# A two-block transformer step: three last blocks turned on VectorE and by DMAs instead of on TensorE

## The chip, the cores and the metric

One NeuronCore of a Trainium2 chip runs one launch of the program. The metric is the device time of the launch in microseconds (us), the median of several runs. The engines are TensorE (PE in the profile, PEld its weight loads), VectorE (DVE), ScalarE (ACT), GpSimd (POOL) and SyncE (SP, which only issues DMAs and waits).

## The reference

The input x has 256 tokens of width 2048, in float32. Two blocks follow each other. Cut to what matters here:

```
# first block
h = rms_norm(x) ;  proj = h @ w_in            # four mixers over proj, 512 columns each
x1 = x + rms_norm_per_mixer(mixed) @ w_out
h = rms_norm(x1, norm_ffn)                    # x1 * rstd * norm_ffn
x2 = x1 + (silu(h @ w_gate) * (h @ w_up)) @ w_down       # 5632 inner columns
# second block
o = attention(x2 @ attn_w_in)                 # x2 enters without a norm
x3 = layer_norm(ALPHA * x2 + (o * silu(g)) @ attn_w_out)
o = retention(x3 @ ret_w_in)                  # 8 heads, 512 value columns each
o = group_norm_per_head(o) * silu(g)
out = layer_norm(ALPHA * x3 + o @ ret_w_out)  # 4096 x 2048
```

Each of x1 * norm_ffn, x2 and o * silu(g) is computed with tokens on the partitions and must be the transposed operand of the next product, with its features on the partitions. They must be turned, block by block of 512 columns (a head of the retention is one such block).

## The kernel before

**Products.** The program is a chain of phases: in1, out1, ffn (11 bodies of 8 chunks), down, in2, out2, ret (4 bodies of 24 chunks), out3. In each, an output block of 512 columns (256 tokens, so two banks of PSUM, `ACC`) is summed over chunks of 512 input rows of the weights. A chunk (1 MB) is loaded by SP into one of four places of `raw`. It is used in two halves. To keep float32 accuracy, each half is split: ScalarE copies it to the shorter type fp32r (`split_hi`, `whi`, L379), VectorE subtracts that from the original (`split_lo`, `wlo`, L386), and TensorE makes three products in place of one (`products`, L406 to L408): 12 matmuls of 512 columns for a half. The other operand lies turned in SBUF, split in the same way (`T1H` and `T1L` for ffn and in2, `T2dH` and `T2dL` for out3).

**Order.** Each engine has its own queue, written out by hand and run in order; semaphores tie them. `whi` and `wlo` have places for four halves, so `split_hi` of half q waits until TensorE has finished half q-4, `split_lo` waits for `split_hi`, and a half's products wait for its `split_lo`. SP loads a chunk when VectorE has split the chunk four before it. The other work of each engine is put between the splits, at a position given by the half's number h (or p). What stands "at h" on ScalarE or VectorE comes behind the split of half h.

**Two ways of turning a block.** The first is TensorE's: `tr_pe` makes four transposes of 128x128 for each of the two token groups into a PSUM bank (L439), `tr_act` copies the bank to the high part (L444), `tr_dve` subtracts for the low part (L448). The second leaves TensorE out: VectorE transposes squares of 32x32 within the block (`dve.transpose`, two instructions, into `sg` or `oS`), then 16 DMAs of 32 KB carry the squares between partition groups (`group_across`, L460, four DMAs for each of r = 0 to 3) into `avT` or `oT`; ScalarE copies the turned block to the high part (`x1_hi`, `turned_hi`), VectorE subtracts for the low part (`x1_lo`, `turned_lo`). The semaphore `sq_dve` counts three for each block turned in this way: two for the squares, one for the low part. `sq_in` and `o_in` count landed DMAs.

**Where each is used.** Of the four blocks of x1, blocks 0 to 2 go the second way with the DMAs on GpSimd's queue; of the four of x2, blocks 0 to 2 with the DMAs on SP's, four before each of four weight loads; so do heads 0 to 6 of the retention. Block 3 of x1, block 3 of x2 and head 7 go the first way: their `tr_pe` stands in TensorE's queue behind half 1 of ffn's first body, behind half 1 of in2 and behind half 5 of out3, which are already products with the blocks before. The products with the last block begin at half 6 of ffn and in2 and at half 14 of out3, where TensorE waits for `tb_done`.

Of the kernel before, what the change touches and what calls it, by code (L numbers as in the profile page):

```python
# [33 lines left out]
P = 128  # L34
# [34 lines left out]
ACROSS = 4 * 4 * 16  # L69
SQ = {"mix": 0, "out1": 2, "ffn": 5, "down": 16, "in2": 19, "ret": 21}  # L70
BY_SP = {"ffn": 0, "down": 11, "ret": 14}

# [20 lines left out]
def two_blocks(nc, A, out):  # L93
# [133 lines left out]
    SML = at("SML", G0 + 18 * KB, [P, 2, T], F32R)  # L227
    oR = at("oR", G0 + 24 * KB, [P, J, W])
    gR = at("gR", G0 + 28 * KB, [P, J, W])
    X4 = at("X4", G0, [P, J, D])  # L230
# [46 lines left out]
    def sem(name):  # L277
# [46 lines left out]
        sem(x) for x in ("r_sq", "r_hi", "r_S", "r_SM", "r_out", "r_ms", "r_rs", "r_norm", "r_og", "r_TL", "r_vH", "r_prod", "r_SMH"))  # L324
    x4_ready, out_st = sem("x4_ready"), sem("out_st")

# [189 lines left out]
    BLK = {"in1": 0, "out1": 11, "ffn": 15, "down": 37, "in2": 41, "out2": 51, "ret": 55, "out3": 79}  # L516
    TB = {"mix": 0, "out1": 4, "down": 6, "in2": 8, "out2": 12, "ret": 20}

# [80 lines left out]
    def _(sp):  # L599
# [29 lines left out]
        for c in range(8):  # L629
            w = A["w_ffn_gate"] if c < 4 else A["w_ffn_up"]  # L630
            load(sp, "ffn", c, [(0, W, chunk(w[0], c % 4, 0))])
        with sp.Fori(1, NF) as f:
# [59 lines left out]
        with sp.Fori(1, RH // 2) as i:  # L692
            ret(i, False)
        for c in range(32):
            load(sp, "out3", c, [(0, W, chunk(A["ret_w_out_2"][0], c % 8, c // 8 * W))])
        n = 0
# [10 lines left out]
    def _(pool):  # L707
# [125 lines left out]
        for hd in range(RH):  # L833
            pool.wait_ge(r_sq, 2 * hd + 2)
            for r in range(2, 4):
                group_across(pool, line3(rb), line4(rTs), r, t_in2)
        pool.wait_ge(tb_done, TB["ret"] + 2)
        pool.dma_start(lnG2[:, :], spread(A["ln_gain_2"][1], D)).then_inc(ln_in, 16)
# [9 lines left out]
    def _(act):  # L848
# [211 lines left out]
        def x1_hi(b):  # L1060
            act.wait_ge(o_in, (b + 1) * ACROSS)
            act.activation(by_token(T1H[:, 4 * b:4 * b + 4, :]), avT[:, :, :, :], ACT.Copy).then_inc(sq_hi, 1)

        for b in range(FB):
            for h in range(8):
                split_hi(act, "out1", 4 * b + h // 2, h % 2)
                if b == 0:
                    if h == 1:
                        mix_rstd(2)
                    if h == 2:  # L1070
                        out1_block(NB1 - 1)
                    mix_hi(h)
                    if h == 3:
                        act.wait_ge(oc_ready, NH)
                        squares(3)
                    if h == 4:
                        mix_rstd(3)
                if b and h == 4:
                    x1_squares(b - 1)
                if b >= 2 and h == 3:  # L1080
                    x1_hi(b - 2)


        def ffn(f, first):
            for h in range(16):
                split_hi(act, "ffn", h // 2, h % 2, i=f)
                if first and h == 2:
                    x1_squares(FB - 1)
                if first and h == 3:
                    x1_hi(2)  # L1090
                    for j in range(J):
                        tr_act(act, TB["out1"] + j, part(T1H, 3, j), k=j)
                if first and h == 4:
                    rstd(rstd2, ms1, 3, rs1)
                    table_silu()
                if not first and h == 13:
                    turned_hi(act, f - 1, T2bH[:, bass.ds(f * 4 - 4, 4), :], avT, f)
                if first and h == 11:

                    act.wait_ge(x1_st[0], 32)  # L1100
                    act.wait_ge(x1_st[1], 32)
                if h == 11:
                    block_done(act, "ffn", 3, f)
                    if not first:

                        act.wait_ge(sq_in, f * ACROSS)
                    for j in range(J):
                        act.activation(sg[:, j, :], ACC[BLK["ffn"] % 2][j], ACT.Silu, scale=rstd2[:, j:j + 1]).then_inc(acc_out[BLK["ffn"] % 2], 1)
# [191 lines left out]
        for b in range(FB):  # L1300
            for h in range(16):
# [4 lines left out]
                if b == 0 and h == 3:  # L1306
# [15 lines left out]
    def _(dve):  # L1322
# [281 lines left out]
        def x1_block(b):  # L1604
# [10 lines left out]
            tt(xgb[:, b % 2, :, :], x1b[:, b % 2, :, :], rep(gF[:, b * W:(b + 1) * W], 0, J), MUL).then_inc(xg2, 1)  # L1615
            if b < FB - 1:
                dve.wait_ge(xg2, b + 1)
                if b:
                    dve.wait_ge(o_in, b * ACROSS)
                for j in range(J):  # L1620
                    dve.transpose(sg[:, j, :], xgb[:, b % 2, j, :]).then_inc(sq_dve, 1)

# [4 lines left out]
        for b in range(FB):  # L1627
            for h in range(8):
# [15 lines left out]
                if b and h == 3:  # L1644
                    x1_block(b - 1)


# [17 lines left out]
        def ffn(f, first):  # L1665
            for h in range(16):
# [26 lines left out]
        def x2_block(b):  # L1693
# [5 lines left out]
            for j in range(J):  # L1699
                tt(x2b[:, j, :], ACC[B % 2][j], xr2[:, j, :], ADD).then_inc(acc_out[B % 2], 1)  # L1700
            if b < FB - 1:
                for j in range(J):
                    dve.wait_ge(acc_out[B % 2], 2 * (B // 2) + 1 + j)
                    dve.transpose(sg[:, j, :], x2b[:, j, :]).then_inc(sq_dve, 1)

# [40 lines left out]
        def in2_at(p):  # L1746
            if p == 0:
                x2_block(FB - 1)
            if p == 3:
                for j in range(J):  # L1750
                    tr_dve(dve, TB["down"] + j, part(T1H, 3, j), part(T1L, 3, j), k=j)
            if p == 7:
# [302 lines left out]
        for b in range(FB):  # L2055
            for h in range(16):
# [5 lines left out]
                if b == 0 and h == 4:  # L2062
# [25 lines left out]
    def _(pe):  # L2088
# [219 lines left out]

        def x1_tr(b):
            pe.wait_ge(xg2, b + 1)  # L2310
            for j in range(J):
                tr_pe(pe, TB["out1"] + j, xgb[:, b % 2, j, :], k=j)

        for b in range(FB):
# [10 lines left out]
        def ffn(f, first):  # L2325
            for h in range(16):
                if first and h == 0:
                    pe.wait_ge(sq_dve, 3 * (SQ["ffn"] - 1))
                if first and h == 4:
                    pe.wait_ge(sq_dve, 3 * SQ["ffn"])  # L2330
                if first and h == 6:
                    pe.wait_ge(tb_done, TB["out1"] + 2)
                products(pe, "ffn", h // 2, h % 2, T1H, T1L, 4 * (h % 8 // 2), BLK["ffn"] + h // 8, W, h % 8 == 0, h % 8 == 7, f)
                if first and h == 1:
                    x1_tr(FB - 1)

# [3 lines left out]


        def x2_tr():
            B = BLK["down"] + FB - 1
            pe.wait_ge(acc_out[B % 2], 2 * (B // 2) + 2)
            for j in range(J):
                tr_pe(pe, TB["down"] + j, x2b[:, j, :], k=j)

# [42 lines left out]
        for p in range(80):  # L2390
            b, h = p // 8, p % 8
            if p == 0:
                pe.wait_ge(sq_dve, 3 * SQ["in2"])
            if p == 6:
                pe.wait_ge(tb_done, TB["down"] + 2)
            products(pe, "in2", p // 2, p % 2, T1H, T1L, 4 * (h // 2), BLK["in2"] + b, W, h == 0, h == 7)
            if p == 1:
                x2_tr()
            in2_at(p)
# [83 lines left out]
        for b in range(FB):  # L2483
            for h in range(16):
                if b == 0 and h == 0:
                    pe.wait_ge(sq_dve, 3 * (SQ["ret"] + RH - 1))
                if b == 0 and h == 14:
                    pe.wait_ge(tb_done, TB["ret"] + 2)
                if b == FB - 1 and h >= 16 - 2 * SPLITS:
                    continue  # L2490
                products(pe, "out3", 8 * b + h // 2, h % 2, T2dH, T2dL, 4 * (h // 2), BLK["out3"] + b, W, h == 0, h == 15)
                if b == 0 and h == 5:
                    pe.wait_ge(r_og, 2 * RH)
                    for j in range(J):
                        tr_pe(pe, TB["ret"] + j, oR[:, j, :], (4, 6), j)
        b = FB - 1
# [79 lines left out]
```

## Time and profile before

| | us |
|---|---|
| median of 3 runs (2189.58 to 2190.57) | 2189.77 |
| span of the profiled execution, first to last instruction | 2187.9 |
| TensorE busy, share of the span | 2175.2, 99% |
| VectorE busy | 1341.7, 61% |
| ScalarE busy | 1039.5, 48% |
| GpSimd busy | 222.5, 10% |
| from HBM | 415.32 MB, 194 GB/s over the span with 8.39 MB written |

The profile gives the profiled execution's own time only as its span; the median of the runs lies 1.9 us above it. Matmuls are pipelined and their ends are modelled, so a busy TensorE is not one at its peak: the distance from one matmul's start to the next tells more. Times of the rows count from the start of the span.

### The profile page before, as it was taken

Reading aid. Unit: us, or ns where it says so; the run is one execution under the profiler, and the core shown is the slowest. Engines: PE = TensorE matmul, PEld = TensorE weight load, DVE = VectorE, ACT = ScalarE, POOL = GpSimd, SP = SyncE. Lnnn points to the kernel's source line nnn. Section 1 sums busy time; section 2 is a strip of 40 time slices with the busy share of each in tenths; the row PEclk is TensorE's granted clock in tenths of the full one; section 3 lists DMA queues with packets and bytes.
Section 4 is the critical chain, followed back from the end, with each engine's and each line's share of the span. In section 5 each row is a group of like instructions: output and inputs, shape, how many; then the busy total and the mean of one; then the engine's idle time right before and its main releaser. Section 6 shows DMA issues by size and latency. Waiting matters only on the chain.

```text
span 2187.9 us, 26695 instructions
## 1 busy us (share of the span) xinstructions
PE 2175.2 (99%) x9999; PEld 1809.9 (83%) x9999; DVE 1341.7 (61%) x1645; ACT 1039.5 (48%) x1292; POOL 222.5 (10%) x376
## 2 busy tenths in 40 slices
PE   9999999999999999999999999999999999999998
PEld 7888888888888888888888888888888888888886
DVE  6675676555555555445566776587666565665556
ACT  6554664444444444444444455445444544544333
POOL 1012015000000000010002352000000000000000
PEclk9999999999999999999999999999999999999999
DMA  9557568676657665676766776757676657756763
GB/s 317 194 162 200 163 221 283 198 217 214 201 184 224 206 201 185 219 227 222 223 210 205 202 211 198 269 197 222 188 212 192 200 186 209 211 170 200 257 204 111
DMA packets 388375, 454.83 MB, mean 208 GB/s; under 512 B 167042, under 2 KB 202274, under 8 KB 387137
## 3 DMA queue, kind: packets, MB, share of 16 engines
q1 hardware_dynamic: 371568, 414.97, 60.6%
q0 software_dynamic: 16432, 38.43, 5.9%
q8 instruction: 55, 0.90, 0.2%
q10 hardware_dynamic: 288, 0.27, 0.0%
q14 instruction: 32, 0.25, 0.0%
HBM read 415.32 MB, written 8.39 MB: 194 GB/s over the span
## 4 chain that ended last, share of the span: by engine, by line
PE 99%; DVE 0%; DMA 0%; SPq 0%; ACT 0%; issue 0%
PE bank L406 30%; PE bank L408 30%; PE bank L407 30%; PE bank L420 1%; PE bank L422 1%; PE bank L421 1%; PE bank L2381 1%; PE bank L2368 1%; PE bank L2154 0%; PE bank L439 0%; PE bank L2477 0%; PE bank L2478 0%; PE bank L2476 0%; PE bank L2139 0%; DMA raw<-in_w_in 0%; PE bank L2218 0%
## 5 line engine op out<-in xcount | busy, mean ns | idle before, releaser
L386 DVE TENSOR_TENSOR wlo<-raw,whi 128x1024 fp32r<-128x1024 f32 x749 | 903.6, 1216 | 681.2 <-ACT whi L379 679.7
L379 ACT ACTIVATE whi<-raw 128x1024 fp32r<-128x1024 f32 x749 | 780.4, 1053 | 777.1 <-PE bank L408 761.3
L406 PE MATMUL bank<-whi,T1H 128*128 128x512 f32 (+1 forms) x2100 | 823.7, 392 | 0.0
L408 PE MATMUL bank<-whi,T1L 128*128 128x512 f32 (+1 forms) x2100 | 814.7, 388 | 0.0
L407 PE MATMUL bank<-wlo,T1H 128*128 128x512 f32 (+1 forms) x2100 | 814.1, 388 | 0.0
L408 PEld LDWEIGHTS bank<-whi,T1L 128*128 128x128 f32 x2100 | 394.2, 188 | 81.6
L406 PEld LDWEIGHTS bank<-whi,T1H 128*128 128x128 f32 x2100 | 394.4, 188 | 79.6 <-DVE wlo L386 0.2
L407 PEld LDWEIGHTS bank<-wlo,T1H 128*128 128x128 f32 x2100 | 394.5, 188 | 79.3
L406 PE MATMUL bank<-whi,T2bH 128*128 128x512 f32 x352 | 136.9, 389 | 0.0
L407 PE MATMUL bank<-wlo,T2bH 128*128 128x512 f32 x352 | 136.9, 389 | 0.0
L408 PE MATMUL bank<-whi,T2bL 128*128 128x512 f32 x352 | 136.9, 389 | 0.0
L406 PE MATMUL bank<-whi,T2dH 128*128 128x512 f32 x224 | 87.2, 389 | 0.0
L408 PE MATMUL bank<-whi,T2dL 128*128 128x512 f32 x224 | 87.1, 389 | 0.0
L407 PE MATMUL bank<-wlo,T2dH 128*128 128x512 f32 x224 | 87.1, 389 | 0.0
L460 POOL DMA_DIRECT2D rTs<-rb x64 | 37.2, 588 | 468.7 <-DVE rb L1999 462.4
L408 PEld LDWEIGHTS bank<-whi,T2bL 128*128 128x128 f32 x352 | 66.1, 188 | 13.8
L407 PEld LDWEIGHTS bank<-wlo,T2bH 128*128 128x128 f32 x352 | 66.1, 188 | 13.7
L406 PEld LDWEIGHTS bank<-whi,T2bH 128*128 128x128 f32 x352 | 66.1, 188 | 13.6
L790 POOL DMA_DIRECT2D scr_x<-x2b x4 | 2.9, 723 | 648.3 <-DVE x2b L1700 648.3
L406 PE MATMUL bank<-whi,T2aH 128*128 128x512 f32 x128 | 50.3, 393 | 0.0
L408 PE MATMUL bank<-whi,T2aL 128*128 128x512 f32 x128 | 49.9, 390 | 0.0
L407 PE MATMUL bank<-wlo,T2aH 128*128 128x512 f32 x128 | 49.8, 389 | 0.0
(406 smaller groups left out, 1843.7 us busy)
## 6 DMA issues: line engine op xcount, KB each, us to landing
raw<-in_ret_w_in SPq DMA_DIRECT2D x64, 1024.0 KB, 5.4
raw<-in_w_ffn_gate SPq DMA_DIRECT2D x44, 1024.0 KB, 5.2
raw<-in_w_ffn_up SPq DMA_DIRECT2D x44, 1024.0 KB, 5.6
raw<-in_w_ffn_down SPq DMA_DIRECT2D x44, 1024.0 KB, 5.7
raw<-in_attn_w_in SPq DMA_DIRECT2D x40, 1024.0 KB, 5.4
raw<-in_w_in SPq DMA_DIRECT2D x39, 1024.0 KB, 5.1
raw<-in_ret_w_in SPq DMA_DIRECT2D x64, 512.0 KB, 4.6
raw<-in_ret_w_out SPq DMA_DIRECT2D x32, 1024.0 KB, 5.1
```

What stands on the lines that cost most here:

```text
L379: eng.activation(hi_[:, s, :, :n], raw[:, c % RAWS, HALF * hf:HALF * (hf + 1), :n], ACT.Copy).then_inc(hi_ready, 1)
L386: eng.tensor_tensor(lo[:, s, :, :n], raw[:, c % RAWS, HALF * hf:HALF * (hf + 1), :n], hi_[:, s, :, :n].bitcast(F32), ALU.subtract).then_in ...
L406: eng.matmul(o, TH[:, kt, xs], hi_[:, s, t, :n], start=first and t == 0, stop=False)
L407: eng.matmul(o, TH[:, kt, xs], lo[:, s, t, :n], start=False, stop=False)
L408: m = eng.matmul(o, TL[:, kt, xs], hi_[:, s, t, :n], start=False, stop=last and t == HALF - 1)
L420: eng.matmul(o, TH[:, kt, xs], hi_[:, s, t, :], start=first and t == 0, stop=False)
L421: eng.matmul(o, TH[:, kt, xs], lo[:, s, t, :], start=False, stop=False)
L422: m = eng.matmul(o, TL[:, kt, xs], hi_[:, s, t, :], start=False, stop=last and t == HALF - 1)
L460: eng.dma_start(dst[:, :, r, :], src[:, :, b, :]).then_inc(landed_, 16)
L790: pool.dma_start(rows(scr_x2)[:, :, cs], x2b[:, :, :]).then_inc(x2_st, 16)
L2368: m = mm(bank[6][:, j * T:(j + 1) * T], qTa[:, g % 2, j, a, :], kTa[:, :, g, :], start=True, stop=True)
L2381: m = mm(bank[(5, 7)[u % 2]][:, j * P:(j + 1) * P], PTa[u // 2 % 2][:, u % 2, j, s, :], vA[:, s, g * P:(g + 1) * P], start=s == 0, stop=s ...
```

## The change

Block 3 of x1, block 3 of x2 and head 7 of the retention are turned the second way. Their `tr_pe`, `tr_act` and `tr_dve` go. VectorE makes the squares behind the block's sum. SP issues all 16 DMAs of a block in one row: ahead of the load of chunk 4 in ffn's first body and in in2, and of chunk 7 in out3. For x1 they count on a semaphore of their own, `x1z_in`. To keep the order of `sq_dve`, the copy and the subtraction of x1's block 2 move from half 3 of ffn's first body to behind the split of out1's last half, and those of block 3 stand at half 3. For x2 the copy stays at p = 3, the subtraction goes to p = 4. For the retention head the squares stand at half 5, copy and subtraction at half 10, and two new tiles, `oSz` and `oTz`, take the squares and the turned block. GpSimd's loads for the last layer norm wait for head 7's subtraction as before, now by `sq_dve`.

```
-SQ = {"mix": 0, "out1": 2, "ffn": 5, "down": 16, "in2": 19, "ret": 21}
-BY_SP = {"ffn": 0, "down": 11, "ret": 14}
+SQ = {"mix": 0, "out1": 2, "ffn": 6, "down": 17, "in2": 21, "ret": 23}
+BY_SP = {"ffn": 0, "down": 11, "ret": 15}
...
+    oSz = at("oSz", G0 + 32 * KB, [P, J, W])
+    oTz = at("oTz", G0 + 36 * KB, [P, J, 4, P])
...
@@ SP
         for c in range(8):
             w = A["w_ffn_gate"] if c < 4 else A["w_ffn_up"]
+            if c == 4:
+                sp.wait_ge(sq_dve, 3 * (SQ["out1"] + FB - 1) + 2)
+                for r in range(4):
+                    group_across(sp, line3(sg), line4(avT), r, x1z_in)
             load(sp, "ffn", c, [(0, W, chunk(w[0], c % 4, 0))])
...
             for cc in range(4):
+                if 4 * b + cc == 4:
+                    for r in range(4):
+                        block_across(sp, SQ["down"] + FB - 1, sg, avT, r)
                 load(sp, "in2", 4 * b + cc, [(0, W, chunk(A["attn_w_in_2"][0], cc, COL2[kind] + g * W))])
...
         for c in range(32):
+            if c == 7:
+                for r in range(4):
+                    block_across(sp, SQ["ret"] + RH - 1, oSz, oTz, r)
             load(sp, "out3", c, [(0, W, chunk(A["ret_w_out_2"][0], c % 8, c // 8 * W))])
@@ GpSimd
-        pool.wait_ge(tb_done, TB["ret"] + 2)
+        pool.wait_ge(sq_dve, 3 * (SQ["ret"] + RH))
@@ ScalarE
         def x1_hi(b):
-            act.wait_ge(o_in, (b + 1) * ACROSS)
+            if b == FB - 1:
+                act.wait_ge(x1z_in, ACROSS)
+            else:
+                act.wait_ge(o_in, (b + 1) * ACROSS)
...
                 if b >= 2 and h == 3:
                     x1_hi(b - 2)
+                if b == FB - 1 and h == 7:
+                    x1_hi(2)
...
                 if first and h == 3:
-                    x1_hi(2)
-                    for j in range(J):
-                        tr_act(act, TB["out1"] + j, part(T1H, 3, j), k=j)
+                    x1_hi(FB - 1)
...
             if p == 3:
-                for j in range(J):
-                    tr_act(act, TB["down"] + j, part(T1H, 3, j), k=j)
+                turned_hi(act, SQ["down"] + FB - 1, T1H[:, 4 * FB - 4:4 * FB, :], avT, BY_SP["down"] + FB)
...
-                if b == 0 and h == 7:
-                    for j in range(J):
-                        tr_act(act, TB["ret"] + j, part(T2dH, RH - 1, j), (4, 6), j)
+                if b == 0 and h == 10:
+                    turned_hi(act, SQ["ret"] + RH - 1, T2dH[:, 4 * RH - 4:4 * RH, :], oTz, BY_SP["ret"] + RH)
@@ VectorE
-            if b < FB - 1:
-                dve.wait_ge(xg2, b + 1)
-                ...
+            dve.wait_ge(xg2, b + 1)
+            if b:
+                dve.wait_ge(o_in, b * ACROSS)
+            for j in range(J):
+                dve.transpose(sg[:, j, :], xgb[:, b % 2, j, :]).then_inc(sq_dve, 1)
...
+                if b == FB - 1 and h == 7:
+                    x1_lo(2)
...
                 if first and h == 3:
-                    x1_lo(2)
-                    for j in range(J):
-                        tr_dve(dve, TB["out1"] + j, part(T1H, 3, j), part(T1L, 3, j), k=j)
+                    x1_lo(FB - 1)
...
-            if b < FB - 1:
-                for j in range(J):
-                    ...
+            for j in range(J):
+                dve.wait_ge(acc_out[B % 2], 2 * (B // 2) + 1 + j)
+                dve.transpose(sg[:, j, :], x2b[:, j, :]).then_inc(sq_dve, 1)
...
-            if p == 3:
-                for j in range(J):
-                    tr_dve(dve, TB["down"] + j, part(T1H, 3, j), part(T1L, 3, j), k=j)
+            if p == 4:
+                turned_lo(dve, SQ["down"] + FB - 1, T1H[:, 4 * FB - 4:4 * FB, :], T1L[:, 4 * FB - 4:4 * FB, :], avT)
...
-                if b == 0 and h == 7:
+                if b == 0 and h == 5:
                     for j in range(J):
-                        tr_dve(dve, TB["ret"] + j, part(T2dH, RH - 1, j), part(T2dL, RH - 1, j), (4, 6), j)
+                        dve.wait_ge(r_og, 2 * RH - 1 + j)
+                        dve.transpose(oSz[:, j, :], oR[:, j, :]).then_inc(sq_dve, 1)
+                if b == 0 and h == 10:
+                    turned_lo(dve, SQ["ret"] + RH - 1, T2dH[:, 4 * RH - 4:4 * RH, :], T2dL[:, 4 * RH - 4:4 * RH, :], oTz)
@@ TensorE: x1_tr, x2_tr and the tr_pe of oR go, and
                 if first and h == 6:
-                    pe.wait_ge(tb_done, TB["out1"] + 2)
...
+                if first and h in (0, 4, 6):
+                    pe.wait_ge(sq_dve, 3 * (SQ["ffn"] - {0: 2, 4: 1, 6: 0}[h]))
...
             if p == 0:
+                pe.wait_ge(sq_dve, 3 * (SQ["in2"] - 1))
+            if p == 6:
                 pe.wait_ge(sq_dve, 3 * SQ["in2"])
-            if p == 6:
-                pe.wait_ge(tb_done, TB["down"] + 2)
...
                 if b == 0 and h == 14:
-                    pe.wait_ge(tb_done, TB["ret"] + 2)
+                    pe.wait_ge(sq_dve, 3 * (SQ["ret"] + RH))
```

## Rows read from the trace of the kernel before

**Rows 1.** The page's first part: busy us, share of the span, instructions.

```profile
PE 2175.2 (99%) x9999; PEld 1809.9 (83%) x9999; DVE 1341.7 (61%) x1645; ACT 1039.5 (48%) x1292; POOL 222.5 (10%) x376
```

**Rows 2.** TensorE's waits, all of them: us in total, times, longest.

```profile
PE bank L2300 <- DVE warm L1581: 1.5, 1, 1.5
PE bank L2114 <- DVE wlo L1578: 0.6, 1, 0.6
```

**Rows 3.** TensorE's timeline around x1's transposes: start, us, instruction, count.

```profile
386.50 0.39 PE L406 MATMUL bank<-whi,T1H 128*128 128x512 f32 x1
...
391.71 0.39 PE L408 MATMUL bank<-whi,T1L 128*128 128x512 f32 x1
391.94 1.03 PE L439 MATMUL bank<-cst,xgb 128*128 128x128 f32 x8
...
395.81 0.39 PE L407 MATMUL bank<-wlo,T1H 128*128 128x512 f32 x1
```

**Rows 4.** ScalarE's timeline, same place: two splits and block 2's copy.

```profile
375.82 1.06 ACT L379 ACTIVATE whi<-raw 128x1024 fp32r<-128x1024 f32 x1 [1.60 <-PE bank L408]
...
384.04 1.06 ACT L379 ACTIVATE whi<-raw 128x1024 fp32r<-128x1024 f32 x1 [1.72 <-PE bank L408]
...
390.59 1.04 ACT L1062 ACTIVATE T1H<-avT 128x1024 fp32r<-128x1024 f32 x1
```

**Rows 5.** VectorE's timeline: block 2's sum, squares, splits, block 3's sum.

```profile
368.31 1.28 DVE L1612 TENSOR_TENSOR x1b<-bank,xrb 128x512 f32<-128x512 f32 x2
...
370.89 1.31 DVE L1621 STREAM_TRANSPOSE sg<-xgb 128x512 f32<-128x512 f32 x2
372.12 3.46 DVE L386 TENSOR_TENSOR wlo<-raw,whi 128x1024 fp32r<-128x1024 f32 x3
...
386.70 1.29 DVE L1612 TENSOR_TENSOR x1b<-bank,xrb 128x512 f32<-128x512 f32 x2 [3.12 <-PE bank L408]
```

**Rows 6.** Block 2's last DMAs on GpSimd's queue, and their landing.

```profile
L460 POOL DMA_DIRECT2D avT<-sg x2: 585/585/585, 380.7 to 381.3; - x2
DMA to landing us min/median/max: 4.2/4.5/4.8
```

**Rows 7.** SP's timeline: a weight load, eight small DMAs, four beside loads; landings; the load's median.

```profile
383.61 0.37 SPq L365 DMA_DIRECT2D raw<-in_w_ffn_up  x1
...
1146.17 5.19 SPq L460 DMA_DIRECT2D qTa<-tS  x8
DMA to landing us min/median/max: 1.9/2.1/2.9
...
1058.23 3.77 SPq L460 DMA_DIRECT2D avT<-sg  x4
DMA to landing us min/median/max: 3.0/4.3/5.0
...
raw<-in_w_ffn_up SPq DMA_DIRECT2D x44, 1024.0 KB, 5.6
```

**Rows 8.** Timelines of VectorE, ScalarE and TensorE where in2 begins.

```profile
1105.70 1.29 DVE L1700 TENSOR_TENSOR x2b<-bank,xr 128x512 f32<-128x512 f32 x2 [5.78 <-PE bank L408]
1105.70 1.06 ACT L379 ACTIVATE whi<-raw 128x1024 fp32r<-128x1024 f32 x1 [1.60 <-PE bank L408]
1108.22 0.45 PE L406 MATMUL bank<-whi,T1H 128*128 128x512 f32 x1
```

**Rows 9.** Timelines of VectorE and TensorE in out3's first block.

```profile
2010.28 1.22 DVE L386 TENSOR_TENSOR wlo<-raw,whi 128x1024 fp32r<-128x1024 f32 x1
2018.69 1.03 PE L439 MATMUL bank<-cst,oR 128*128 128x128 f32 x8
```

**Rows 10.** Warm-up matmuls (ns min/median/max, starts), and windows: granted clock after PE's busy time.

```profile
L2300 PE MATMUL bank<-warm x6: 592/866/1222, 1.5 to 5.1; 128*128 128x512 f32 x6
...
2178.00:2180.00 2.00, 0.00 (x0) 1.00 0.00 0
2182.00:2182.20 0.20, 0.00 (x0) 0.64 0.97 369
```

More of the change, by code:

```diff
@@ L324, in two_blocks @@
         sem(x) for x in ("r_sq", "r_hi", "r_S", "r_SM", "r_out", "r_ms", "r_rs", "r_norm", "r_og", "r_TL", "r_vH", "r_prod", "r_SMH"))
-    x4_ready, out_st = sem("x4_ready"), sem("out_st")
+    x4_ready, out_st, x1z_in = sem("x4_ready"), sem("out_st"), sem("x1z_in")
     class Chain:
@@ L516, in two_blocks @@
     BLK = {"in1": 0, "out1": 11, "ffn": 15, "down": 37, "in2": 41, "out2": 51, "ret": 55, "out3": 79}
-    TB = {"mix": 0, "out1": 4, "down": 6, "in2": 8, "out2": 12, "ret": 20}
+    TB = {"mix": 0, "out1": 4, "in2": 4, "out2": 8}
     def where1(c):
@@ L1615, in x1_block @@
             tt(xgb[:, b % 2, :, :], x1b[:, b % 2, :, :], rep(gF[:, b * W:(b + 1) * W], 0, J), MUL).then_inc(xg2, 1)
-            if b < FB - 1:
-                dve.wait_ge(xg2, b + 1)
-                if b:
-                    dve.wait_ge(o_in, b * ACROSS)
-                for j in range(J):
-                    dve.transpose(sg[:, j, :], xgb[:, b % 2, j, :]).then_inc(sq_dve, 1)
+            dve.wait_ge(xg2, b + 1)
[3 more added lines that the diff above has]
+                dve.transpose(sg[:, j, :], xgb[:, b % 2, j, :]).then_inc(sq_dve, 1)
         def x1_lo(b):
@@ L1700, in x2_block @@
                 tt(x2b[:, j, :], ACC[B % 2][j], xr2[:, j, :], ADD).then_inc(acc_out[B % 2], 1)
-            if b < FB - 1:
-                for j in range(J):
-                    dve.wait_ge(acc_out[B % 2], 2 * (B // 2) + 1 + j)
-                    dve.transpose(sg[:, j, :], x2b[:, j, :]).then_inc(sq_dve, 1)
+            for j in range(J):
+                dve.wait_ge(acc_out[B % 2], 2 * (B // 2) + 1 + j)
+                dve.transpose(sg[:, j, :], x2b[:, j, :]).then_inc(sq_dve, 1)
         for b in range(FB):
@@ L1748, in in2_at @@
                 x2_block(FB - 1)
-            if p == 3:
-                for j in range(J):
-                    tr_dve(dve, TB["down"] + j, part(T1H, 3, j), part(T1L, 3, j), k=j)
+            if p == 4:
+                turned_lo(dve, SQ["down"] + FB - 1, T1H[:, 4 * FB - 4:4 * FB, :], T1L[:, 4 * FB - 4:4 * FB, :], avT)
             if p == 7:
@@ L2306, in _ @@
             mix_tr(p - 8 * NB1)
[L2309 to L2312, printed above, removed]
         for b in range(FB):
@@ L2326, in ffn @@
             for h in range(16):
[L2327 to L2331, printed above, removed]
-                    pe.wait_ge(tb_done, TB["out1"] + 2)
+                if first and h in (0, 4, 6):
+                    pe.wait_ge(sq_dve, 3 * (SQ["ffn"] - {0: 2, 4: 1, 6: 0}[h]))
                 products(pe, "ffn", h // 2, h % 2, T1H, T1L, 4 * (h % 8 // 2), BLK["ffn"] + h // 8, W, h % 8 == 0, h % 8 == 7, f)
-                if first and h == 1:
-                    x1_tr(FB - 1)
         ffn(0, True)
@@ L2339, in _ @@
             ffn(f, False)
[L2342 to L2346, printed above, removed]
         for b in range(FB):
@@ L2392, in _ @@
             if p == 0:
+                pe.wait_ge(sq_dve, 3 * (SQ["in2"] - 1))
+            if p == 6:
                 pe.wait_ge(sq_dve, 3 * SQ["in2"])
-            if p == 6:
-                pe.wait_ge(tb_done, TB["down"] + 2)
             products(pe, "in2", p // 2, p % 2, T1H, T1L, 4 * (h // 2), BLK["in2"] + b, W, h == 0, h == 7)
-            if p == 1:
-                x2_tr()
             in2_at(p)
@@ L2491, in _ @@
                 products(pe, "out3", 8 * b + h // 2, h % 2, T2dH, T2dL, 4 * (h // 2), BLK["out3"] + b, W, h == 0, h == 15)
[L2492 to L2495, printed above, removed]
         b = FB - 1
```

## The prediction, made before the changed kernel was run

> **What bounds the kernel now.** I read the page's first part, then TensorE's waits, then the timeline of each engine around the three places that change. TensorE is busy for 99% of the span [rows 1], but that share is modelled, so the second view matters more: in the whole execution it waits twice, 2.1 us in all, both at the start [rows 2]. The timeline says the same in another way. From 386.50 to 391.71 there are 24 matmul starts, 0.2265 us apart [rows 3], and this spacing holds nearly everywhere. A half chunk is 12 matmuls, so 2.72 us. So everything that leaves TensorE's stream is won, and everything that makes a half's `wlo` late is lost.
>
> How near is that lateness? `whi`/`wlo` hold four halves. ScalarE's split of half q waits until TensorE has finished q-4, VectorE's follows, and both queues are in order. Between blocks these engines idle, so they look free; but whatever stops one of them for more than about three halves (8 us), less its own work, stops TensorE. That is the measure for all that follows.
>
> **What leaves TensorE.** Eight transposes at each of three places. At x1, 391.71 to 395.81 is 4.10 us [rows 3]; the 14 intervals without the transposes would take 3.17, so they cost 0.93. The other two groups have the same shape (1.03 us for eight in [rows 9]), so I take 0.9 each: 2.7 us in all, 0.12% of the time. That is the most the change can give. What is gone from ScalarE and VectorE (two half-size copies and two subtractions each) is replaced by one full-size copy (1.04) and one subtraction (1.22), and counts as nothing: on those engines it is the same amount of work and lies between splits.
>
> **Place A, x1.** Three waits come in, in a row.
>
> First, block 2. Its copy `x1_hi(2)` moves from half 3 of the ffn phase to behind the split of out1's last half, which ScalarE issues at 375.82 [rows 4]. There it waits for GpSimd's 16 DMAs, whose last is issued at 381.3 and lands 4.2 to 4.8 us later [rows 6]: 385.8. Before, it ran at 390.59 with nothing to wait for [rows 4]. Behind it on ScalarE stand the splits of ffn halves 0, 1 and 2, which had run ahead (the third at 384.04). So: copy to 386.85, split 0 (1.06) to 387.9; on VectorE `x1_lo(2)` to 388.1, `wlo` 0 (1.23) to 389.3. TensorE started that half at 386.50 [rows 3], so it stands 2.8 us. `wlo` 1 ends at 390.5.
>
> Second, block 3's squares. `x1_block(3)` started at 386.70 and now starts at 390.5. With transposes it takes 3.81 us to the next split (368.31 to 372.12, block 2) [rows 5], so `wlo` 2 ends at 395.5. TensorE has gone through halves 0 and 1 by 389.3 + 5.4 = 394.7: 0.8 us more.
>
> Third, the DMAs. SP waits for the squares, 3.9 us after 390.5, at 394.4, and issues 16 DMAs before the load of chunk 4. Eight such issues take 5.19 us, 0.65 each, and land in 1.9 to 2.9 (median 2.1) where no weight load is under way [rows 7]; here the loads before have landed and the next stand behind. Last issue starts 15 x 0.65 = 9.75 later, landing at 406.3. ScalarE has stood in `x1_hi(3)` since split 3, and split 4 is queued behind it: copy to 407.3, split to 408.4; `x1_lo(3)` to 408.5 and `wlo` 4 to 409.7 on VectorE. TensorE has finished half 3 at 401.0 and stands for 8.7 us. Before, half 4 began at 395.81 + 11 x 0.2265 = 398.3. Place A: +11.4 us, the saved transposes included. Chunk 4 is issued at about 405 instead of 383.61 and its half 8 is wanted four halves after 409.7, at 420; a load lands in 5.6 us [rows 7], so that is covered.
>
> **Place B, x2.** `x2_block(3)` starts at 1105.70 on VectorE [rows 8], and TensorE's half 1 began at 1108.22, just behind its `wlo`. Two transposes (1.31) [rows 5] before that split make it late by about 1.3. SP starts at 1105.70 + 1.29 + 1.31 = 1108.3; the last DMA starts at 1118.0 and lands at 1120.1. ScalarE had issued split 3 at 1105.70 [rows 8] and now stands in the copy, splits 4 and on behind it. Copy to 1121.2, split 4 to 1122.3, `wlo` 4 to 1123.5 (`turned_lo` comes after it here). Before, half 4 began at 1108.22 + 36 x 0.2265 + 0.9 for the transposes = 1117.3. Place B: +6.2 us, of which 5.9 is one stand.
>
> **Place C, the retention head.** `wlo` of half 5 runs at 2010.28 [rows 9]; the squares follow to 2012.8, the DMAs in quiet land at 2012.8 + 9.75 + 2.1 = 2024.7. The copy stands behind split 10, and TensorE wants half 11 at 2018.69 + 5 x 2.72 = 2032.3; the copy, the subtraction and `wlo` 11 take 3.5, so a landing before 2028.8 costs nothing. That is 4 us of room: -0.9. But chunk 6 is being loaded just then. With a load beside them four issues took 3.77 (0.94 each) and landed up to 5.0 us later [rows 7]; so 2031.9, and 3.1 us lost. I take the first; the second is a bound.
>
> **The clock.** After its last matmul TensorE was still granted full clock in 2178 to 2180, and the clock fell near 2182.1 [rows 10], with no matmul in between. At the start the same plain fp32 matmul record is 592 to 1222 ns, and the slow ones run from 1.48 to some 4.3 us [rows 10]. So stands of 8.7 and 5.9 us can bring 1.2 GHz, and about 2.8 us of work then goes at half speed, losing 1.4 each time: +2.8. Bounds: nothing, if the clock stays, and 2 us each. The Trainium skill ("TensorE: Matmul & The Clock Gate", "Part 1: The HAM clock gate") has the same two levels, with idle time lowering the clock and sustained work restoring it; by it both stands cost as the rows say, and a sum without it is 2.8 lower.
>
> **Sum.** 11.4 + 6.2 - 0.9 + 2.8 = +19.5 us. Span 2187.9 + 19.5 = 2207.4. The profile gives no time of that execution but its span; the median of the runs lies 1.9 above, and I keep that: 2209.3, slower by 0.89%.
>
> **Rivals.**
> *All covered (0.04).* The DMAs land before the copies need them. For B this needs a landing by 1114.2, 6 us after the squares; for A 2.9 us after them, and block 2 by 383. Against it: 16 issues alone take 9 to 10 us. Even then B keeps its 1.3 us of transposes ahead of `wlo` 1 against the 0.9 saved: -0.9 + 0.4 - 0.9 - a rest near zero gives 2188.4. Not slower, and within what a measurement tells.
> *Cheap issues (0.06).* SP's issue of a weight load takes 0.37 [rows 7]. If the small ones, queued 16 in a row, went at that pace, the last starts 5.6 after the squares: A +7.2, B +2.0, C -0.9, and the clock perhaps once: 2189.8 + 8.3 + 1.4 = 2199.5. Against it are the eight in 5.19. The Trainium skill ("DMA: Bandwidth & Descriptors", "Issuing engines are not separate DMA queues") goes further: issuing is usually small beside the DMA itself. Taken so, only the landing would count, A would be about +2.5 and B +0.4, in all 2191.8; the rows have 0.65 per issue, sixteen times, against one landing of 2.1, so they disagree with it.
> *Crowded DMAs (0.12).* 0.94 per issue and 5 us of landing at all three places: A and B +7.3 each, C +4.0: 2228 at the very most; a part of it is likelier, 2217 to 2222. For it: such rows exist; against it: at A and B the loads are held back by the same SP queue. GpSimd's store of the block (512 KB) is the only other traffic.
> *Forecast (0.78)*: both places stand on the turning, issues near 0.65, with or without the clock.
>
> **Numbers.** A measurement of this kernel tells about 0.2% (4.4 us) from no change. Within the forecast: no clock loss 2206.5; issues at 0.585 and landing in 1.9 take 1.2 from each place, 2204.1; clock at 2 each and 1.5 us more landing each give 2213.5; a part of C's loss 2216. Range 2203 to 2216: it leaves out the first two rivals and most of the third, at most 2 in 10. Faster would take more than the 2.7 us that exist: 0.01. Same: 0.05. Slower: 0.94.
>
> **What the profile after would show.** No L439 rows with xgb, x2b or oR; L460 on SP with 16 in a row at each place; TensorE's waits with three or four new entries: about 3 us before ffn half 0, 1 before half 2, 9 before half 4 and, in in2, 1.3 before half 1 and 6 before half 4; ScalarE waiting for the DMAs at the copies; a granted clock below 1.00 for a few us after both long stands; nothing at C. I am wrong if the copies find their data landed, if ScalarE's splits reach half 4 without them, or if C shows a wait.

## The result, and the profile after

The changed kernel takes 2210.14 us (median of 4 runs, 2209.7 to 2210.49) against 2189.98 for the kernel before on the same chip: a ratio of 1.0092, 95% interval 1.0079 to 1.0104, 20.2 us. The prediction was 2209.3, range 2203 to 2216. The span went from 2187.9 to 2208.5 us.

The page's first part and TensorE's waits of the kernel after, against [rows 1, 2]:

```profile
PE 2179.0 (99%) x9975; PEld 1810.7 (82%) x9975; DVE 1344.5 (61%) x1648; ACT 1039.0 (47%) x1289; POOL 221.6 (10%) x376
...
PE bank L408 <- DVE wlo L388: 17.6, 4, 8.5
PE bank L2313 <- DVE warm L1594: 1.5, 1, 1.5
```

The busy share still says 99%. The new line of waits says the rest: four times, 17.6 us, TensorE stood for a `wlo`, so for the second half of a weight split, and never for a turned block. So something further back in the queues of ScalarE and VectorE held the splits up. (Of the lines that carry the split and the products before, L379, L386 and L406 to L408 are now L381, L388 and L408 to L410; `group_across` is L462.)

**x1.** TensorE's timeline, against [rows 3]:

```profile
386.42 0.39 PE L410 MATMUL bank<-whi,T2aL 128*128 128x512 f32 x1
388.93 0.47 PE L408 MATMUL bank<-whi,T1H 128*128 128x512 f32 x1 [2.12 <-DVE wlo L388]
...
401.29 0.39 PE L410 MATMUL bank<-whi,T1L 128*128 128x512 f32 x1
410.17 0.76 PE L408 MATMUL bank<-whi,T1H 128*128 128x512 f32 x1 [8.49 <-DVE wlo L388]
410.73 0.63 PE L409 MATMUL bank<-wlo,T1H 128*128 128x512 f32 x1
```

Half 0 of ffn begins at 388.93, half 4 at 410.17. Before, half 4 began at 398.30 and the last matmul of out1 at 386.27:

```profile
386.27 0.39 PE L408 MATMUL bank<-whi,T2aL 128*128 128x512 f32 x1
...
398.30 0.39 PE L406 MATMUL bank<-whi,T1H 128*128 128x512 f32 x1
```

What held it is read backwards, from ScalarE's, VectorE's and SP's timelines (one fence for each; against [rows 4, 5, 7]):

```profile
375.97 1.06 ACT L381 ACTIVATE whi<-raw 128x1024 fp32r<-128x1024 f32 x1 [1.60 <-PE bank L410]
385.33 1.06 ACT L1077 ACTIVATE T1H<-avT 128x1024 fp32r<-128x1024 f32 x1 [8.30 <-DMA avT<-sg]
386.29 2.93 ACT L381 ACTIVATE whi<-raw 128x1024 fp32r<-128x1024 f32 x3
...
392.74 1.06 ACT L381 ACTIVATE whi<-raw 128x1024 fp32r<-128x1024 f32 x1
406.57 1.06 ACT L1077 ACTIVATE T1H<-avT 128x1024 fp32r<-128x1024 f32 x1 [12.77 <-DMA avT<-sg]
407.54 1.04 ACT L381 ACTIVATE whi<-raw 128x1024 fp32r<-128x1024 f32 x1
```

```profile
389.83 1.28 DVE L1625 TENSOR_TENSOR x1b<-bank,xrb 128x512 f32<-128x512 f32 x2
...
407.66 1.23 DVE L485 TENSOR_TENSOR T1L<-avT,T1H 128x1024 fp32r<-128x1024 f32 x1 [11.43 <-ACT T1H L1077]
408.80 1.22 DVE L388 TENSOR_TENSOR wlo<-raw,whi 128x1024 fp32r<-128x1024 f32 x1
```

```profile
393.74 11.50 SPq L462 DMA_DIRECT2D avT<-sg  x16
405.29 9.90 SPq L367 DMA_DIRECT2D raw<-in_w_ffn_up  x4
```

ScalarE waits twice in front of a copy, 8.30 us for block 2's DMAs and 12.77 us for block 3's. Behind the first stand three splits (386.29, x3), behind the second split 4 (407.54), on which `wlo` 4 (408.80) and TensorE (410.17) depend. Between the two copies lie the 16 issues on SP, 11.50 us, from 393.74; a change of order on the other engines doesn't shorten them.

**x2.** VectorE, SP, ScalarE and TensorE where in2 begins, against [rows 8]:

```profile
1119.15 1.29 DVE L1712 TENSOR_TENSOR x2b<-bank,xr 128x512 f32<-128x512 f32 x2 [5.78 <-PE bank L410]
1121.68 10.91 SPq L462 DMA_DIRECT2D avT<-sg  x16
1133.92 1.06 ACT L481 ACTIVATE T1H<-avT 128x1024 fp32r<-128x1024 f32 x1 [13.71 <-DMA avT<-sg]
...
1122.81 0.50 PE L408 MATMUL bank<-whi,T1H 128*128 128x512 f32 x1 [0.98 <-DVE wlo L388]
1137.24 0.79 PE L408 MATMUL bank<-whi,T1H 128*128 128x512 f32 x1 [5.97 <-DVE wlo L388]
```

The same chain, with a short stand before half 1 (the two transposes ahead of `wlo` 1) and the long one before half 4.

**The retention head.** SP's and ScalarE's timelines, VectorE's at the start of out3, and below them the landings from the view of the tile `oTz`:

```profile
2034.23 10.44 SPq L462 DMA_DIRECT2D oTz<-oSz  x16
...
2046.01 1.06 ACT L481 ACTIVATE T2dH<-oTz 128x1024 fp32r<-128x1024 f32 x1 [1.77 <-DMA oTz<-oSz]
...
2021.34 1.23 DVE L388 TENSOR_TENSOR wlo<-raw,whi 128x1024 fp32r<-128x1024 f32 x1
```

```profile
DMA to landing us min/median/max: 1.9/1.9/4.1
```

ScalarE waits 1.77 us there too, but it had run ahead, and TensorE has no wait.

The same instruction in both traces gives the size of each place. TensorE's last matmul of out1 starts 0.15 later than before (386.42 against 386.27). The sum of x2's block 3 starts at 1119.15 against 1105.70, an offset of 13.45: so x1 cost 13.3. The split at 2021.34 stood at 1999.83 before, an offset of 21.51: x2 cost 8.1. At the end the offset is 20.6: the retention head gave 0.9. The split before, in VectorE's timeline:

```profile
1999.83 1.22 DVE L386 TENSOR_TENSOR wlo<-raw,whi 128x1024 fp32r<-128x1024 f32 x1
```

### The profile page after: what moved, and what is told of

It is laid out like the page before. It is cut to its first block, busy times and chain, and to the rows that moved or that the text cites. A ratio compares the mean times of both kernels' runs of the same rounds, so it can differ in the third digit from the quotient of the medians.

```text
span 2208.5 us, 26693 instructions
## 1 busy us (share of the span) xinstructions
PE 2179.0 (99%) x9975; PEld 1810.7 (82%) x9975; DVE 1344.5 (61%) x1648; ACT 1039.0 (47%) x1289; POOL 221.6 (10%) x376
## 4 chain that ended last, share of the span: by engine, by line
PE 97%; DVE 1%; SPq 1%; POOL 0%; DMA 0%; issue 0%; ACT 0%; DVEq 0%; ACTq 0%
PE bank L408 29%; PE bank L410 29%; PE bank L409 29%; SPq L462 1%; PE bank L422 1%; PE bank L424 1%; PE bank L423 1%; PE bank L2377 1%; PE bank L2364 1%; PE bank L2167 0%; POOL avT L462 0%; DMA avT<-sg 0%; PE bank L2472 0%; PE bank L2471 0%; PE bank L2470 0%; PE bank L2152 0%
## 5 line engine op out<-in xcount | busy, mean ns | idle before, releaser
L388 DVE TENSOR_TENSOR wlo<-raw,whi 128x1024 fp32r<-128x1024 f32 x749 | 903.1, 1216 | 686.3 <-ACT whi L381 685.1
L381 ACT ACTIVATE whi<-raw 128x1024 fp32r<-128x1024 f32 x749 | 780.1, 1053 | 774.5 <-PE bank L410 762.1
L408 PE MATMUL bank<-whi,T1H 128*128 128x512 f32 (+1 forms) x2100 | 826.0, 393 | 17.6 <-DVE wlo L388 17.6
L410 PE MATMUL bank<-whi,T1L 128*128 128x512 f32 (+1 forms) x2100 | 816.3, 389 | 0.0
L408 PEld LDWEIGHTS bank<-whi,T1H 128*128 128x128 f32 x2100 | 395.6, 188 | 98.8 <-issue 11.4
L410 PEld LDWEIGHTS bank<-whi,T1L 128*128 128x128 f32 x2100 | 395.0, 188 | 82.3
L408 PE MATMUL bank<-whi,T2bH 128*128 128x512 f32 x352 | 136.9, 389 | 0.0
L410 PE MATMUL bank<-whi,T2bL 128*128 128x512 f32 x352 | 136.9, 389 | 0.0
L408 PE MATMUL bank<-whi,T2dH 128*128 128x512 f32 x224 | 87.1, 389 | 0.0
L410 PE MATMUL bank<-whi,T2dL 128*128 128x512 f32 x224 | 87.1, 389 | 0.0
L462 POOL DMA_DIRECT2D rTs<-rb x64 | 37.0, 586 | 468.7 <-DVE rb L2009 462.5
L408 PEld LDWEIGHTS bank<-whi,T2bH 128*128 128x128 f32 x352 | 66.1, 188 | 13.8
L410 PEld LDWEIGHTS bank<-whi,T2bL 128*128 128x128 f32 x352 | 66.1, 188 | 13.7
L408 PE MATMUL bank<-whi,T2aH 128*128 128x512 f32 x128 | 50.3, 393 | 0.0
L410 PE MATMUL bank<-whi,T2aL 128*128 128x512 f32 x128 | 49.9, 390 | 0.0
```

The source lines that it names most:

```text
L381: eng.activation(hi_[:, s, :, :n], raw[:, c % RAWS, HALF * hf:HALF * (hf + 1), :n], ACT.Copy).then_inc(hi_ready, 1)
L388: eng.tensor_tensor(lo[:, s, :, :n], raw[:, c % RAWS, HALF * hf:HALF * (hf + 1), :n], hi_[:, s, :, :n].bitcast(F32), ALU.subtract).then_in ...
L408: eng.matmul(o, TH[:, kt, xs], hi_[:, s, t, :n], start=first and t == 0, stop=False)
L410: m = eng.matmul(o, TL[:, kt, xs], hi_[:, s, t, :n], start=False, stop=last and t == HALF - 1)
L462: eng.dma_start(dst[:, :, r, :], src[:, :, b, :]).then_inc(landed_, 16)
```

## The experiments

**One place at a time.** Three kernels, each with the new way at one place and TensorE's way at the other two (the counts in `SQ`, `BY_SP` and `TB` go with it). A part of the first, on TensorE, against the kernel after:

```
 # x1 only: x2 and the retention head as in the kernel before
+            if p == 1:
+                B = BLK["down"] + FB - 1
+                pe.wait_ge(acc_out[B % 2], 2 * (B // 2) + 2)
+                for j in range(J):
+                    tr_pe(pe, TB["down"] + j, x2b[:, j, :], k=j)
...
+                if b == 0 and h == 5:
+                    pe.wait_ge(r_og, 2 * RH)
+                    for j in range(J):
+                        tr_pe(pe, TB["ret"] + j, oR[:, j, :], (4, 6), j)
```

> Only block 3 of x1 is turned by squares and DMAs; x2's last block and head 7 are turned by TensorE as before. In the trace after, TensorE had lost 13.3 us between the start of ffn and the end of down (the same VectorE instruction at 1105.70 before and 1119.15 after, less 0.15 of an earlier shift). Theory (the three places are independent, each with its own stand of TensorE): 2190.0 + 13.3 = 2203.3 us. Rival (the places share something, the DMA queue or the clock, so that they don't add): more than 1 us away from that, with the sum of the three single runs away from the whole change's +20.2.

> Only block 3 of x2 is turned by squares and DMAs. In the trace after, this place lost 8.1 us (an offset of 13.45 before it and 21.51 behind it). Theory (independent places): 2190.0 + 8.1 = 2198.1 us. Rival (not independent): more than 1 us away from it.

> Only head 7 of the retention is turned by squares and DMAs. Theory (its turning is wholly hidden, and eight transposes leave TensorE's stream at 0.9 us): 2190.0 - 0.9 = 2189.1 us, no wait of TensorE in out3. Rival (what TensorE no longer does is filled by something else, or the crowded weight loads behind SP's 16 DMAs cost it): 2190.0 or above.

Measured against 2190.0 us: x1 alone 2203.08 (ratio 1.0059, 1.0044 to 1.0075), x2 alone 2198.68 (1.0039, 1.0023 to 1.0054), the head alone 2189.34 (0.9997, 0.9988 to 1.0006). In us: +13.1, +8.7, -0.7. They sum to 21.1 against 20.2 of the whole change, with runs of one kernel up to 2 us apart. The places are independent within that. The head's gain is not told from nothing by its times. That it costs no wait is seen in TensorE's list, which holds the start alone:

```profile
PE bank L2307 <- DVE warm L1585: 1.5, 1, 1.5
```

**The clock.** Only matmuls are added, into a bank that nobody reads:

```
+                if first and h == 4:           # 34 in ffn; the same with 22 at p == 4 in in2
+                    for k in range(34):
+                        pe.matmul(bank[4], T1H[:, 0, 0:P], T1H[:, 2:4, :].rearrange("p a t -> p (a t)"), start=True, stop=True)
                 products(pe, "ffn", h // 2, h % 2, T1H, T1L, ...)
```

> The whole change, and 34 more matmuls of 512 columns on TensorE before ffn's half 4, 22 before in2's half 4, into a bank that nobody reads; they take 7.7 and 5.0 us and fit into the stands of 8.7 and 6.1 us. Theory (of each long stand about 1.65 us is not waiting but work at the lower clock afterwards: eight starts 0.43 apart in place of 0.23): 2210.1 - 3.3 = 2206.8 us, and a granted clock of 1.00 behind both. Rival (the slow matmuls behind the stands cost nothing because VectorE's and ScalarE's catching up sets the pace there anyway): 2210.1.

Measured: 2206.93 us (1.0079, 1.0063 to 1.0094), 3.2 below the change. Windows of TensorE, first after, then this kernel (columns: us, PE busy and count, granted clock, DMA share, GB/s):

```profile
402.00:410.00 8.00, 0.00 (x0) 0.78 0.60 158
410.00:414.00 4.00, 3.83 (x10) 0.58 0.84 282
```

```profile
402.00:410.00 8.00, 6.65 (x29) 1.00 0.65 188
410.00:414.00 4.00, 4.00 (x19) 1.00 0.77 230
```

In the kernel after, the granted clock falls from full to 1.2 GHz (0.50) late in this stand: it is 1.00 in 405.0 to 406.5 and 0.50 from 406.5 on. From 410 to 414 the kernel after holds 10 matmul starts, this one 19. The tenth matmul of half 4 in the kernel after, whose first is at 410.17, then the first and the tenth of this kernel:

```profile
413.78 0.40 PE L408 MATMUL bank<-whi,T1H 128*128 128x512 f32 x1
```

```profile
409.43 0.50 PE L408 MATMUL bank<-whi,T1H 128*128 128x512 f32 x1 [1.35 <-DVE wlo L388]
...
411.61 0.39 PE L408 MATMUL bank<-whi,T1H 128*128 128x512 f32 x1
```

The nine intervals take 3.61 us, and the same 3.61 behind x2's stand (1137.24 to 1140.85); with the clock kept they take 2.18. So the clock costs 1.4 us at each place, 2.9 of the 20.2, and that is not waiting. The spans of the two profiled executions differ by 3.7: the 2.9, and 0.7 by which half 4 itself began sooner (409.43 against 410.17).

**The copies two halves later.** Nothing but the place of two calls on each engine moves:

```
-                if first and h == 3:
+                if first and h == 5:
                     x1_hi(FB - 1)      # ScalarE; x1_lo on VectorE the same
...
-            if p == 3:                 # ScalarE; on VectorE p == 4
+            if p == 5:
```

> The whole change, but ScalarE's copy and VectorE's subtraction of the last block stand at half 5 in ffn's first body and at p = 5 in in2, in place of 3 (and 4). Nothing else moves; TensorE needs the block at half 6. Theory (the stand comes from the splits 4 and 5 queued behind a copy whose data is under way): x1's copy begins with the landing as before (406.5), so TensorE stands before half 6 for 3.2 us in place of 8.7 before half 4, in2's for 0.8 in place of 6.1; with the clock kept 1.65 less each: 2210.1 - 5.5 - 5.3 - 3.3 = 2196 us (2199 if the clock falls anyway). Rival (TensorE stands for its operand, the turned block, and not for the splits): no change, 2210.

Measured: 2198.57 us (1.0038, 1.0025 to 1.0051), 11.6 less than the change. The rival is out: the operand was not what TensorE stood for before half 4. The time lies between the theory's two numbers (2196 with the clock kept, 2199 if it falls). The clock did fall at x1: it is 0.50 in 411.5 to 413.0. ScalarE's copy in its timeline, and TensorE's longest line of waits:

```profile
406.66 1.06 ACT L1077 ACTIVATE T1H<-avT 128x1024 fp32r<-128x1024 f32 x1 [7.84 <-DMA avT<-sg]
```

```profile
PE bank L408 <- DVE wlo L388: 8.7, 5, 4.4
```

The copy runs when it ran before, at 406.66, but splits 4 and 5 are done. The stand before half 6 is 4.4 and not the 3.2 expected, because TensorE came to it sooner: it had no stand before half 4 and, in this execution, no low clock behind the first stand.

**Two queues for the DMAs.**

```
-                for r in range(4):
+                for r in range(2):
                     group_across(sp, line3(sg), line4(avT), r, x1z_in)
...
+        pool.wait_ge(sq_dve, 3 * (SQ["out1"] + FB - 1) + 2)     # GpSimd; x2 alike
+        for r in range(2, 4):
+            group_across(pool, line3(sg), line4(avT), r, o_in)
```

> The whole change, but at x1 and x2 SP issues 8 of the 16 DMAs and GpSimd the other 8. Copies and subtractions stay. Theory (the turning is long because one queue needs 0.65 to 0.7 us for each of 16 issues; the landing is 2 us): the last lands 5 us earlier at both places, so the stands are 3.7 and 1.1 us and the clock may hold: 2210.1 - 10 - 3 = 2197 us (2200 with the clock falling at x1). Rival (the small copies share the same DMA engines, so that issuing them from two queues gives nothing): 2210.

Measured: 2200.91 us (1.0045, 1.0029 to 1.006), 9.2 less, near the 2200 expected if the clock falls at x1, which it did. So most of the turning's length was issue time on the one queue. The copy at x2 runs 9.83 us after the sum's start (1126.01, 1116.18) in place of 14.77, 4.9 sooner as expected; by the offsets x2 gave 6.4 of the time, the clock there being kept, and x1 3.0. At x1 the gain is 2.9 us of landing and not 5. SP's, GpSimd's and ScalarE's timelines there, and the landing of SP's eight:

```profile
393.73 5.70 SPq L462 DMA_DIRECT2D avT<-sg  x8
399.47 10.53 SPq L367 DMA_DIRECT2D raw<-in_w_ffn_up  x3
...
393.99 4.63 POOL L462 DMA_DIRECT2D avT<-sg  x8 [1.87 <-DVE sg L1643]
398.70 0.73 POOL L799 DMA_DIRECT2D xr<-scr_x  x1
...
403.65 1.06 ACT L1085 ACTIVATE T1H<-avT 128x1024 fp32r<-128x1024 f32 x1 [9.86 <-DMA avT<-sg]
```

```profile
DMA to landing us min/median/max: 1.9/2.4/4.8
```

The last of SP's eight starts at 398.8 and lands 4.8 later, beside a weight load (399.47, in the kernel after at 405.29) and GpSimd's load of `xr` (398.70, in the kernel after at 395.11). The one comes sooner because SP has eight issues less ahead of it, the other later because GpSimd has eight more. With all 16 on SP no load ran beside the last ones and they landed in 1.9. That the loads are the cause is argued from the trace; no run takes them away.

**Block 2's copy put back.**

```
-                if b == FB - 1 and h == 7:
-                    x1_hi(2)                # ScalarE; x1_lo(2) on VectorE
...
                 if first and h == 2:
+                    x1_hi(2)
                     x1_squares(FB - 1)
...
                 if first and h == 1:
+                    x1_lo(2)
                     x1_block(FB - 1)
```

> The whole change, but the copy and subtraction of x1's block 2 stand behind the splits of ffn's half 2 (ScalarE) and half 1 (VectorE), in place of behind out1's last split. Theory (this moved step holds three splits, makes a first stand of 2.3 us and starts block 3's squares 1.6 us late): the first stand is gone and the squares come 1.6 us earlier, so that all behind them does: 2210.1 - 1.6 = 2208.5 us. Rival (all stands add, and the first one's 2.3 us with its slow matmuls come back whole): 2206 or less.

Measured: 2209.37 us (1.0089, 1.0074 to 1.0105), 0.8 less, where the theory had 1.6 and the rival 4 or more: the rival is out by the time. The first stand is gone, and half 4 of ffn begins at 407.37 in place of 410.17, 2.8 sooner. The stand before it has grown, though, and the stretch at low clock behind it is longer. TensorE's waits, half 4, and the window behind it:

```profile
PE bank L408 <- DVE wlo L388: 16.4, 4, 9.1
```

```profile
407.37 0.77 PE L408 MATMUL bank<-whi,T1H 128*128 128x512 f32 x1 [9.10 <-DVE wlo L388]
```

```profile
407.00:414.00 7.00, 6.63 (x18) 0.57 0.86 302
```

Thirteen intervals are long there, against seven in the kernel after, and ten against seven behind x2's stand. So of the 2.8 us 1.6 are left by in2 and 0.9 at the end. The 0.8 of the medians is no larger than the spread of the runs. The run also doesn't tell by size what the 2.8 us are: block 3's sum starts 2.4 sooner, and the stand that went was 2.3 long.

**All three repairs.** The above together, and two places more: x1's turned block goes to a place of its own, so that its DMAs start with the squares and need not wait until `avT` is read, and x2's squares stand behind the split of half 1.

```
+    xTz = at("xTz", FT + 8 * KB, [P, J, 4, P])
...
-                sp.wait_ge(sq_dve, 3 * (SQ["out1"] + FB - 1) + 2)
+                sp.wait_ge(sq_dve, 3 * (SQ["out1"] + FB - 1) + 1)
-                for r in range(4):
-                    group_across(sp, line3(sg), line4(avT), r, x1z_in)
+                for r in range(2):
+                    group_across(sp, line3(sg), line4(xTz), r, x1z_in)
...
             if p == 0:
                 x2_block(FB - 1)
+            if p == 1:
+                x2_squares(FB - 1)
```

> The whole change with the three repairs together: DMAs of x1's and x2's last blocks half on SP and half on GpSimd, their copies and subtractions at half 5, block 2's copy at half 2 and subtraction at half 2, x1's turned block in a place of its own so that its DMAs start with the squares, and x2's squares behind the split of half 1. Theory (each turning is then covered by halves 0 to 5, and only the 24 transposes' 2.7 us are left): no wait of TensorE at any of the three places, 2190.0 - 2.6 = 2187.4 us. Rival (some 1 us stand remains at x1, where VectorE has 3.8 us of sum and squares to do between two splits): 2188.5 to 2190.

Measured: 2188.67 us against 2189.86 (0.9995, 0.9985 to 1.0004), not told from the kernel before. The number is the rival's (2188.5 to 2190) and not the theory's (2187.4): a stand of 0.9 was left. But it stands before ffn's half 6 (402.62 to 403.74, where 0.23 is the spacing), and not where VectorE has sum and squares to do. ScalarE and VectorE there:

```profile
400.14 1.06 ACT L1086 ACTIVATE T1H<-xTz 128x1024 fp32r<-128x1024 f32 x1 [2.93 <-DMA xTz<-sg]
401.11 1.99 ACT L382 ACTIVATE whi<-raw 128x1024 fp32r<-128x1024 f32 x2
...
401.23 1.23 DVE L486 TENSOR_TENSOR T1L<-xTz,T1H 128x1024 fp32r<-128x1024 f32 x1 [2.76 <-ACT T1H L1086]
402.38 2.35 DVE L389 TENSOR_TENSOR wlo<-raw,whi 128x1024 fp32r<-128x1024 f32 x2
```

Split 6 is behind the copy once more. So one place further:

```
-                if first and h == 5:
+                if first and h == 6:
                     x1_hi(FB - 1)      # and x1_lo on VectorE
```

> As the kernel with all three repairs, but x1's last copy and subtraction stand at half 6 in place of half 5, so that split 6 goes ahead of the wait for the DMAs. There TensorE still stood 0.9 us before ffn's half 6: the copy ran at 400.14, behind it split 6, and wlo 6 ended at 403.6, wanted at 402.8. Theory (that stand is the queue order on ScalarE and VectorE again): split 6 and wlo 6 are done by 399.6, the subtraction by 402.5, no stand is left, 2188.7 - 0.9 = 2187.8 us, faster than the kernel before by 0.1%. Rival (the DMAs' landing itself is too late for half 6): a stand of the same size, 2188.7.

Measured: 2187.8 us (11 runs, 2187.17 to 2188.51) against 2190.09: 0.9989, 0.998 to 0.9998. The stand before half 6 went, and 0.9 us with it, as expected. This version is faster than the kernel before, by 0.11%, and so than the kernel after. ScalarE's timeline, then TensorE's waits:

```profile
396.30 2.01 ACT L382 ACTIVATE whi<-raw 128x1024 fp32r<-128x1024 f32 x2
400.81 1.06 ACT L1086 ACTIVATE T1H<-xTz 128x1024 fp32r<-128x1024 f32 x1 [2.51 <-DMA xTz<-sg]
```

```profile
PE bank L2330 <- DVE warm L1604: 1.5, 1, 1.5
PE bank L2144 <- DVE wlo L1601: 0.5, 1, 0.5
PE bank L409 <- DVE wlo L389: 0.2, 1, 0.2
```

The copy came later than in the version before it (400.81 against 400.14), and TensorE still stands for only 0.2 us.

## Why the prediction was right

The forecast's likeliest case is what happened, and both long stands came before the half that it named. That the sum is right to 0.7 us is in part luck, as the items on the turning and on the clock show.

| | predicted | measured |
|---|---|---|
| x1, clock included | 11.4 + 1.4 | 13.3 by offset, 13.1 alone |
| x2, clock included | 6.2 + 1.4 | 8.1 by offset, 8.7 alone |
| retention head | -0.9 | -0.9 by offset, -0.7 alone |
| both stands' clock (in the rows above) | 2.8 | 2.9 by the intervals |
| sum | 19.5 | 20.2 by the medians, 20.6 by the spans |

- *Block 2's copy.* Forecast at 385.8, a first stand of 2.8. It ran at 385.33, the stand was 2.3 (386.65 to 388.93). The prediction reads it as one chain with the second long stand: what counts is then the 3.1 us by which block 3's sum starts late (389.83 against 386.70), and not the stand's own length. The trace bears the chain out, since the later stand grew by 0.6 when this one went; but the two lengths are too near each other for the run with block 2's copy put back to tell them apart.
- *The second stand*, 0.8 before half 2, is not in this trace: the clock had fallen after the first, and TensorE came to half 2 at 396.07, with `wlo` 2 done at about 394.9. With x1 alone the clock held, and a stand was there, half as long as forecast (a gap of 0.62, 0.4 above the spacing).
- *The turning.* Forecast: 10.4 us of issues from 394.4, landing at 406.3. The trace has 11.50 us from 393.74, and the copy at 406.57. The start was 0.7 sooner and the row of issues 1.1 longer than forecast, and the two nearly cancel. Splitting the issues over two queues took 9.2 us from the time, so the issues were most of the length.
- *Who stands behind the copy.* Forecast: splits 4 and on. Moving the copies by two halves, with no DMA moved, took 11.6 us. So it was the order in two queues, and not the turned block itself, that held half 4.
- *Chunk 4's late load* cost nothing, as forecast: no wait of TensorE in ffn's first body lies behind half 4.
- *The retention head.* Forecast: the copy's data at 2024.7, against a need by 2028.8. In the kernel after everything here stands 21.5 later, so that is 2046.2; they landed by 2046.0. The bound of 3.1 us for loads beside it was not needed: with three weight loads issued just ahead the 16 issues still took 10.44, and the DMAs landed in 1.9 at the median.
- *The clock* was sized at 1.4 for each stand, from the start of the kernel before, and measured 1.4. That it agrees so closely is luck: seven intervals were long behind either stand, but eleven with x1 alone (410.27 to 415.10 for the eleven, some 2.2 us lost) and fourteen with x2 alone (1123.65 to 1129.77, some 2.8 lost). The first stand's own fall of the clock was not forecast; it lies inside the chain and costs nothing.
- Of the rivals, all covered needed the repairs that the last kernels make; its own price, 2188.4, lies 0.6 from what the last of them took. Cheap issues fell with the 0.65 to 0.72 us from one issue to the next, 16 in a row; a weight load's issue is no measure for a small copy's. The Trainium skill's page "DMA: Bandwidth & Descriptors" ("Issuing engines are not separate DMA queues") says that starting DMAs from several engines saves only the issue time, which is usually small beside the DMA. The first half agrees with the two-queue kernel; the second doesn't hold for 16 copies of 32 KB, 11.5 us of issues against a landing of 1.9. Crowded DMAs came only in part: with all 16 on SP the first few of a row landed in 3.5 to 4.1 us, but the last, which counts, in 1.9; with two queues at x1 the last took 4.8.

## What to carry to other kernels

Work taken off the engine that bounds the kernel can be paid for in latency on others, and the price hangs on what is queued behind the wait as well as on how long the new work takes. Here taking out 2.7 us of transposes cost 20 us. With the copies moved two or three places down their queues, the DMAs split over two queues and the squares and block 2's copy better placed, the same idea gained 2.3 us. Before such a change, count how far ahead the feeding engines are (about three halves, 8 us here) and put the wait behind the last piece of work that may still go ahead of it. Where several waits lie in one chain, mending the first moves the others, and only the last one's end counts: without its first stand of 2.3 us this kernel took only 0.8 less.

## What the runs showed that was not expected

- A short stand may or may not cost the clock. In the kernel after, TensorE stood for 2.1 us before ffn's half 0, and the next matmuls started 0.43 us apart until 392.5 (granted clock 0.66 in 388.0 to 392.5). With x1 alone it stood 2.86 us at the same place, and the clock was 1.00 in 386.5 to 389.0 and in 389.5 to 393.0. In the kernel after the fall came when TensorE was at work again: the clock was still 1.00 in 388.9 to 389.2, and 0.50 in 389.5 to 391.0.
- The stretch at 1.2 GHz behind a stand differs from run to run: seven long intervals behind x1's stand in the kernel after, thirteen in the one with block 2's copy put back. At 0.2 us for each that alone is 1.2 us. Some kernels with stands also spread more, 2.5 us for the late copies (5 runs) and 4.7 us for the two queues (4 runs), against 1.2 us in 16 runs of the kernel before; the kernel after itself doesn't (0.8 in 4). The fastest run of the two queues, 2196.87, has a mean granted clock of 0.998 and the others 0.996 to 0.997, so there the clock may be the reason; no run shows it.
- With no other traffic (399 to 405 in the kernel after) each 32 KB copy between partition groups landed 1.9 us after its issue, and an issue took 0.61 us. The three rows of 16 issues took 10.44, 10.91 and 11.50 us; in the two longer ones one issue near the start took 1.13 and 1.62.
